# The output tiles of two attention stages are transposed into another PSUM bank

## The reference

```
h = rms_norm(x, norm1_g)
split(h @ w_in) -> inputs of four token mixers A, B, C, D, and four gates
A: windowed attention, 8 heads, |i - j| <= 128, with a sink logit
B: differential attention, 4 head pairs, then rms_norm
C: dilated attention, three patterns, combined by their softmax sums
D: latent attention, 8 heads of 96, all 512 keys
merged = sum_i sigmoid(gate_i) * (o_i @ w_branch[i])
x = x + merged @ w_o
u = depthwise_conv(rms_norm(x, norm2_g) @ ffn_w_up)      # width 3
x = x + (silu(u_gate) * u_up) @ ffn_w_down
```

## Time and profile before

| | |
|---|---|
| median of 3 runs | 2765.69 us (2764.04 to 2766.17) |
| profiled execution | 2764.04 us |
| its span, first to last instruction | 2762.3 us |
| PE busy | 2646.5 us, 96% |
| DVE busy | 1567.6 us, 57% |
| ACT busy | 1220.2 us, 44% |
| mean granted TensorE clock | 0.993 |

### The profile page before, as it was taken

One profiled execution on the slowest core, in us unless ns is written; L12 is line 12 of the kernel. 1 busy time (PEld: TensorE's weight loads), 2 busy tenths in 40 slices (PEclk: granted clock), 3 DMA queues, 4 the chain that ended last, 5 costly groups with the idle time before them and its releaser, 6 DMA issues.

```text
span 2762.3 us, 44344 instructions
## 1 busy us (share of the span) xinstructions
PE 2646.5 (96%) x12974; PEld 2218.7 (80%) x12974; DVE 1567.6 (57%) x3240; ACT 1220.2 (44%) x2489; POOL 1.5 (0%) x6
## 2 busy tenths in 40 slices
PE   5999999999999989999979999999999999899999
PEld 4899987777877768888868999877788777788887
DVE  5464577544566556464654545775355566464745
ACT  4455455444544334242435555544445443343423
POOL 0000000000000000000000000000000000000000
PEclk9999999999999999999999999999999999999999
DMA  5212223222121323333332122231221213233332
GB/s 165 77 47 85 81 63 88 66 70 77 54 77 47 100 82 95 99 100 96 96 105 73 54 78 79 72 92 54 69 77 55 76 47 108 84 94 98 94 97 100
DMA packets 144171, 225.99 MB, mean 82 GB/s; under 512 B 15081, under 2 KB 69691, under 8 KB 143035
## 3 DMA queue, kind: packets, MB, share of 16 engines
q1 hardware_dynamic: 133771, 200.83, 24.6%
q10 hardware_dynamic: 10160, 22.24, 2.4%
HBM read 210.39 MB, written 12.65 MB: 81 GB/s over the span
## 4 chain that ended last, share of the span: by engine, by line
PE 79%; DVE 9%; issue 5%; ACT 5%; ACTq 1%; DVEq 1%; DMA 0%; SPq 0%
PE bank L511 61%; PE bank L703 5%; PE bank L541 5%; PE bank L693 5%; DVE s_wl L1297 2%; PE bank L747 1%; ACT s_wh L843 1%; PE bank L738 1%; PE bank L569 1%; ACT s_work L1111 1%; DVE s_gTl L1635 0%; DVE s_work L1397 0%; DMA s_raw<-in_w_in 0%; ACT s_work L872 0%; ACT s_work L874 0%
## 5 line engine op out<-in xcount | busy, mean ns | idle before, releaser
L1297 DVE TENSOR_TENSOR s_wl<-s_raw,s_wh 128x1024 fp32r<-128x1024 f32 (+2 forms) x376 | 453.8, 1208 | 421.6 <-ACT s_wh L843 418.6
L843 ACT ACTIVATE s_wh<-s_raw 128x1024 fp32r<-128x1024 f32 (+2 forms) x376 | 392.5, 1044 | 480.3 <-PE bank L511 443.9
L511 PE MATMUL bank<-s_hTh,s_wh 128*128 128x512 f32 x1216 | 520.3, 428 | 0.0
L511 PE MATMUL bank<-s_hTh,s_wl 128*128 128x512 f32 x1216 | 475.0, 391 | 0.0
L511 PE MATMUL bank<-s_hTl,s_wh 128*128 128x512 f32 x1216 | 474.4, 390 | 0.0
L511 PE MATMUL bank<-s_wh,s_hTh 128*128 128x512 f32 (+1 forms) x1088 | 468.8, 431 | 4.7 <-DVE s_early L1394 4.7
L511 PE MATMUL bank<-s_wh,s_hTl 128*128 128x512 f32 (+1 forms) x1088 | 426.0, 392 | 0.0
L511 PE MATMUL bank<-s_wl,s_hTh 128*128 128x512 f32 (+1 forms) x1088 | 425.2, 391 | 0.0
L1111 ACT ACTIVATE s_work<-s_work,s_stat 128x128 f32<-128x128 f32 (+3 forms) x320 | 167.5, 524 | 266.4 <-DVE s_work L1794 116.1
L511 PEld LDWEIGHTS bank<-s_hTl,s_wh 128*128 128x128 f32 x1216 | 229.0, 188 | 66.6 <-issue 24.4
L511 PEld LDWEIGHTS bank<-s_hTh,s_wh 128*128 128x128 f32 x1216 | 228.8, 188 | 66.8 <-issue 23.4
(11 more groups left out here) (184 smaller groups left out, 3331.0 us busy)
## 6 DMA issues: line engine op xcount, KB each, us to landing
s_raw<-in_w_in SPq DMA_DIRECT2D x168, 512.0 KB, 3.6
s_raw<-in_ffn_w_up SPq DMA_DIRECT2D x176, 256.0 KB, 3.0
s_raw<-in_ffn_w_down SPq DMA_DIRECT2D x44, 512.0 KB, 3.7
s_raw<-in_w_branch SPq DMA_DIRECT2D x32, 512.0 KB, 3.7
s_raw<-in_w_o SPq DMA_DIRECT2D x16, 512.0 KB, 3.8
x_keep<-s_work ACTq DMA_DIRECT2D x2, 2048.0 KB, 7.2
s_raw<-in_w_in SPq DMA_DIRECT2D x16, 256.0 KB, 3.0
gate_keep<-s_early ACTq DMA_DIRECT2D x4, 1024.0 KB, 4.3
```

Of the source, the lines that this page charges most:

```text
L511: last = mm(PJ[b][:, 0:width], st, mv, start=i == 0 and n == 1, stop=i == ntiles - 1 and n == 3 * chunks)
L843: a(wh[:, k % 3, 0:n], raw[:, s, 0:n], ACT.Copy).then_inc(*hi_split.up(own))
L1297: v.tensor_tensor(wl[:, k % 3, 0:n], raw[:, k % 2, 0:n], wh[:, k % 3, 0:n].bitcast(F32), ALU.subtract).then_inc(*tile_split.up(own))
```

## The change

The output tiles of D and A go through bank 6 (TA) in place of bank 5 (TD): PE waits for `ta_act` and `ta_dve` and raises `ta_ready`, ACT and DVE take their group from TA and raise `ta_act` and `ta_dve`. The totals move by eight from td to ta (77 to 69, 128 to 136). The counts on which br3a and br0a wait become ta counts (84 and 120), by a new function `out_turned` that is `turned` for the other pair of counters. The count of turns before B's scores and pads becomes 65, since the seven output tiles that lay between are no longer counted there, and B_OUT 69. DVE's `att_group` waits for `ta_ready` and `ta_act` where `group` waited for `td_act` alone.

```diff
-... td_ready=77, td_act=77, td_dve=77, ... ta_ready=128, ta_act=128, ta_dve=128, ...
+... td_ready=69, td_act=69, td_dve=69, ... ta_ready=136, ta_act=136, ta_dve=136, ...
-D_OUT, A_OUT, B_HEADS, B_OUT = 61, 73, 72, 77
+D_OUT, A_OUT, B_OUT = 84, 120, 69
...
+            def out_turned(n):
+
+                def first(i, b):
+                    if i == 0 and b == 0:
+                        pe.wait_ge(*ta_act.at(l, n))
+                        pe.wait_ge(*ta_dve.at(l, n))
+                return first
...
-                yield from block("br3a", 2, features_out(G), pj_dve, first=turned(D_OUT))
+                yield from block("br3a", 2, features_out(G), pj_dve, first=out_turned(D_OUT))
...
-                yield from block("br0a", 2, features_out(G, first=4), pj_dve, first=turned(A_OUT))
+                yield from block("br0a", 2, features_out(G, first=4), pj_dve, first=out_turned(A_OUT))
...
                         pe.wait_ge(*o_out.at(l, outs + tile + 1))
-                        pe.wait_ge(*td_act.at(l, n_turn[0]))
-                        pe.wait_ge(*td_dve.at(l, n_turn[0]))
-                        n_turn[0] += 1
-                        transposed(TD, tile_of(tile), td_ready)
+                        pe.wait_ge(*ta_act.at(l, n_att[0]))
+                        pe.wait_ge(*ta_dve.at(l, n_att[0]))
+                        n_att[0] += 1
+                        transposed(TA, tile_of(tile), ta_ready)
...
-                yield from attention_b(b_scores, heads_in(B_HEADS, 96))
+                yield from attention_b(b_scores, heads_in(65, 96))
...
-                        hi_out(gTh[:, tile_at:tile_at + 4, P * t:P * t + P], group(), td_act)
+                        hi_out(gTh[:, tile_at:tile_at + 4, P * t:P * t + P], att_group(), ta_act)
...
-                yield from tiles_of("B", qT, B_HEADS, by_map)
+                yield from tiles_of("B", qT, 65, by_map)
...
-                        lo_out(gTl[:, tile_at:tile_at + 4, cols], gTh[:, tile_at:tile_at + 4, cols], group(), td_dve)
+                        lo_out(gTl[:, tile_at:tile_at + 4, cols], gTh[:, tile_at:tile_at + 4, cols], att_group(), ta_dve)
```

More of the change, by code:

```diff
@@ L119 @@
     raw_landed0=120, raw_landed1=120, hi_split=188, tile_split=188, tile_used=134, pj_ready=216, pj_act=108,
-    pj_dve=108, sq_used=60, normed=53, combined=4, sublayer_normed=4, h_normed=8, td_ready=77, td_act=77, td_dve=77, nt_ready=16, nt_act=16,
-    nt_dve=16, ta_ready=128, ta_act=128, ta_dve=128, q_padded=64, s_ready=144, s_biased=144, p_ready=144, b_mixed=16, o_ready=128, o_out=24,
+    pj_dve=108, sq_used=60, normed=53, combined=4, sublayer_normed=4, h_normed=8, td_ready=69, td_act=69, td_dve=69, nt_ready=16, nt_act=16,
+    nt_dve=16, ta_ready=136, ta_act=136, ta_dve=136, q_padded=64, s_ready=144, s_biased=144, p_ready=144, b_mixed=16, o_ready=128, o_out=24,
     gains_in=1, ssum=16, lam_dot=1, lam_exp=1, c_diff=2, c_exp=2, merged_sum=24, merged_hi=8, merged_lo=8, conv_mid=44,
```

## The result

The changed kernel takes 2788.62 us (median of 4 runs, 2784.49 to 2789.34) against 2765.46 for the kernel before, a ratio of 1.0082 with a 95% interval of 1.0063 to 1.0099: 23.2 us slower. 2785 was forecast, within 2774 to 2794. The profiled execution took 2788.19 us with a span of 2786.4, 24.1 over the span before.

A forecast was written before the change was run, and what follows sets the result against it. PE, busy 2646.5 of 2762.3 us, was taken to bound the kernel. Six stalls sum to 9.43 us a layer, 18.9 in two layers; added to the median before this gives 2784.6, stated as 2785, range 2774 to 2794.

The forecast's parts named there:

- No gain from freeing bank 5: In D and A nobody waits for output tiles sharing bank 5 with the head turns; gain 0.
- Nobody's order changes, nothing is added to PE and ACT: No engine's order changes, PE and ACT get no instruction, no transfer moves; DVE gets eight waits more per layer.
- The wait for the probabilities' copies is not added to the next: A's second tile: PE waits some 0.4 us for DVE's copy, without shifting its resumption after the remainder; stall stays 1.98.
- Each stall is the end of DVE's remainder plus 0.06, less PE's old start: Next probability transposes wait for DVE's tile read: D 0.81, 1.77, 1.54; A 1.26, 1.98, 2.07; 9.43 us a layer.
- Zero at the fourth tiles: Fourth tiles of D and A cost 0: br3a and br0a already wait for the remainder, br0a 1.59 us.
- No absorption and no knock-on: Existing waits neither shrink (rival, 2775, chance 0.10) nor do late transposes delay ACT and DVE (rival, 2794, chance 0.10).
- The clock stays at 1.00: Windows D and A keep full clock; rival: ten of twelve stalls lose 1.8 us each, 18 more, 2803, chance 0.04.
- PE's busy time within 2 us: Over the whole span, PE's busy time should stay within 2 us of 2646.5.
- the 0.16 us of the prediction: Profile counts PE idleness from the previous transpose's modelled end, some 0.16 us less than the difference of starts.
- The changed kernel's waits: PE transposes' waits for DVE's remainder rise from 12 to about 24 times, from 7.3 us to some 24.

The follow-up runs named there:

- wait-alone kernel: Kernel before, tiles still in bank 5, PE's probability transposes behind a D or A output tile also wait for the tile's two readers; 2794.48 us, ratio 1.0109.
- two halves: Changed kernel with the bank change made for one mixer only, the other's tiles staying in bank 5: D alone 2774.10 us, A alone 2777.41 us.
- doubled remainder: Changed kernel with DVE computing the remainder of each D and A output tile twice, only the second raising ta_dve; 2812.85 us, ratio 1.0169.

## Why the prediction was right

- *No gain from freeing bank 5.* Held: the old waits of the stretch are the same to a tenth in number and length.
- *Nobody's order changes, nothing is added to PE and ACT.* Held; the counts are equal.
- *The wait for the probabilities' copies is not added to the next.* Held: at the second tile of A the two together cost 2.11 us for 1.98, not 2.4.
- *Each stall is the end of DVE's remainder plus 0.06, less PE's old start.* Held at all six places within 0.13 us, in total 9.68 for 9.43 a layer. The terms that are somewhat too small are the second and third tile of A. The wait-alone kernel, the two halves and the doubled remainder show this wait to be the cause.
- *Zero at the fourth tiles.* Held: br0a waits 1.59 us as before, br3a not at all.
- *No absorption and no knock-on.* Held: the other waits of the stretch did not change, and the losses of D and A add up to the whole.
- *The clock stays at 1.00.* Failed in part. I gave the fall 0.04 as a rival for ten stalls at once, with 1.8 us each, and took the 1.59 us wait before br0a as the argument against it. It comes behind two of twelve, and costs 1.6 us each, 3.3 us: nearly all of the difference between 18.9 and what the stretch lost. The size of one was right, the assumption that it is all or none was not. And there was a nearer row than br0a's in the trace of the kernel before, which I passed over: a wait of 2.92 us ahead of C's output turns, with a fall 1.3 us after PE's return (the wait and a fall are there again in the second layer):

```profile
418.22 0.44 PE L511 MATMUL bank<-s_wh,s_gTh 128*128 128x384 f32 x1 [2.92 <-ACT s_work L874]
```

```profile
418.00:419.50 1.50, 1.28 (x7) 1.29 (x8) 1.25 (x2) 1.50 (x4) 0.00 (x0) 1.00 0.38 145
419.50:422.90 3.40, 3.40 (x13) 3.40 (x12) 3.35 (x5) 1.92 (x4) 0.00 (x0) 0.51 0.00 0
```

A single wait was followed by a fall here, and the fall began only when PE had been back at full rate for a while. The stretch that I had read for br0a, 656 to 799 us, ends 0.6 us after PE's return and could not have shown a later fall; there is none behind it either, but that row did not say so.
- *PE's busy time within 2 us.* Failed: 7.6 more. Slow matmuls count as busy, so the two falls bring 3.3 of it, and the fall at 363 us most of the 1.7 that is there before D begins. But 1.3 us arise in D and A of the first layer, where the clock is 1.00 throughout: where a run of transposes is cut in two, the profile counts the modelled tail of each part as busy (the 0.16 us of the prediction), and this was left out.
- *The changed kernel's waits.* 24 times and some 24 us were forecast; 24 and 23.5 came.

The Trainium skill (TensorE: Matmul & The Clock Gate, What's actually happening) says that an idle engine falls back to 1.2 GHz. The traces agree that it can happen here, behind waits of 1.59 and 1.38 us, but not that it must: the twin waits of the first layer had no fall.

## What to carry to other kernels

A bank that is written, read by two engines in turn and written again costs PE the whole chain, here 0.6 to 2 us, unless PE has other work in its queue before the second write; moving that work ahead of it recovered 19 of 23 us. Price such a wait from the rows as the end of the last reader less the old start of the next writer, place by place, and allow for the clock beside it: here 2 of 12 such waits brought a fall of 1.6 us each, and with waits some 0.8 us longer 8 of 12 did. Look for the same pattern in what is already there: a second bank is worth it where the other bank is idle, but only as far as the next producer keeps up.

## What was not expected of the hardware

Granted clock: 1.2 GHz appeared behind PE waits as short as 1.38 us, after a stretch of full-rate work in between, and not behind equal waits in the other layer. With waits of up to 2.7 us in the doubled-remainder kernel 14 of 25 us are left for it by subtraction, more than the waits' own growth of 10.8. And in the kernel with two further semaphore waits queued behind the one that holds PE, seven of the twelve stalls were longer by 0.16 to 0.20 us; no run tests that cause apart.
